# Experts: the inner-layer transposes and down products of a pair of blocks follow the next pair's gate and up products

## The reference, cut to what matters

```
def hier_moe(h, ...):            # N = 512 tokens, D = 1024, 2 experts each
    ... weight, eid = two best experts of the token's best group ...
    def expert_block(xb, e):
        return (silu(xb @ w_gate_e[e]) * (xb @ w_up_e[e])) @ w_down_e[e]   # 1024 -> 256 -> 1024
    y = sum over a token's two experts of weight * its row of the result
```

## Time and profile before

| | us |
|---|---|
| median of 3 runs | 3019.61 (3017.83 to 3027.75) |
| the profiled execution's own time | 3024.23 |
| its span | 3022.1 |

### The profile page before, as it was taken

One profiled execution on the slowest core, in us unless ns is written; L12 is line 12 of the kernel. 1 busy time (PEld: TensorE's weight loads), 2 busy tenths in 40 slices (PEclk: granted clock), 3 DMA queues, 4 the chain that ended last, 5 costly groups with the idle time before them and its releaser, 6 DMA issues.

```text
span 3022.1 us, 37947 instructions
## 1 busy us (share of the span) xinstructions
PE 2911.9 (96%) x15110; PEld 2272.2 (75%) x15110; DVE 1380.2 (46%) x2211; ACT 901.5 (30%) x1433; POOL 284.1 (9%) x318
## 2 busy tenths in 40 slices
PE   8999999999989999999999999999999988999995
PEld 7888888877846888888888888888888855864442
DVE  5646343545587565564333365333332277521113
ACT  4212111232176322223222244222233255321111
POOL 1000000001100100001000031000010155012221
PEclk9999999999999999999999999999999989999998
DMA  7232323221000365553222232232232200548985
GB/s 282 106 129 101 133 103 127 87 77 56 29 1 15 128 256 189 196 196 105 94 87 102 84 114 70 90 104 98 84 115 97 90 29 1 186 159 355 366 355 233
DMA packets 78350, 395.02 MB, mean 131 GB/s; under 512 B 17552, under 2 KB 19984, under 8 KB 51472
## 3 DMA queue, kind: packets, MB, share of 16 engines
q1 hardware_dynamic: 66704, 384.87, 34.4%
q0 software_dynamic: 11520, 8.43, 0.9%
HBM read 443.56 MB, written 16.78 MB: 152 GB/s over the span
## 4 chain that ended last, share of the span: by engine, by line
PE 90%; DVE 5%; ACT 2%; issue 1%; DMA 1%; POOL 1%; SPq 0%; DVEq 0%; ACTq 0%; POOLq 0%
PE ps L881 17%; PE ps L882 17%; PE ps L883 17%; PE ps L3176 5%; PE ps L3198 3%; PE ps L2210 2%; PE ps L2211 2%; PE ps L2212 2%; PE ps L1583 2%; PE ps L1602 1%; PE ps L1261 1%; PE ps L1262 1%; PE ps L1263 1%; PE ps L2972 1%; PE ps L2973 1%
## 5 line engine op out<-in xcount | busy, mean ns | idle before, releaser
L881 PE MATMUL ps<-h_high_ffn,weights_high_ffn 128*128 128x512 f32 (+1 forms) x1696 | 623.7, 368 | 1.9 <-DVE weights_low_ffn L1036 1.9
L882 PE MATMUL ps<-h_low_ffn,weights_high_ffn 128*128 128x512 f32 (+1 forms) x1696 | 623.8, 368 | 0.0
L883 PE MATMUL ps<-h_high_ffn,weights_low_ffn 128*128 128x512 f32 (+1 forms) x1696 | 623.3, 368 | 0.0
L881 PEld LDWEIGHTS ps<-h_high_ffn,weights_high_ffn 128*128 128x128 f32 x1696 | 320.1, 189 | 55.1 <-issue 2.4
L883 PEld LDWEIGHTS ps<-h_high_ffn,weights_low_ffn 128*128 128x128 f32 x1696 | 320.0, 189 | 52.7
L882 PEld LDWEIGHTS ps<-h_low_ffn,weights_high_ffn 128*128 128x128 f32 x1696 | 320.1, 189 | 52.2
L983 ACT ACTIVATE weights_high_ffn<-weights 128x2048 fp32r<-128x2048 f32 (+4 forms) x160 | 243.9, 1524 | 328.1 <-PE ps L883 263.7
L1036 DVE TENSOR_TENSOR weights_low_ffn<-weights,weights_high_ffn 128x2048 fp32r<-128x2048 f32 (+4 forms) x160 | 289.7, 1811 | 78.0 <-ACT weights_high_ffn L983 76.9
L881 PE MATMUL ps<-hidden_high_ffn,weights_high_ffn 128*128 128x512 f32 (+1 forms) x836 | 309.9, 371 | 0.8 <-DVE weights_low_ffn L1036 0.8
L882 PE MATMUL ps<-hidden_low_ffn,weights_high_ffn 128*128 128x512 f32 (+1 forms) x836 | 309.6, 370 | 0.0
L883 PE MATMUL ps<-hidden_high_ffn,weights_low_ffn 128*128 128x512 f32 (+1 forms) x836 | 309.4, 370 | 0.0
(11 more groups left out here) (479 smaller groups left out, 4499.8 us busy)
## 6 DMA issues: line engine op xcount, KB each, us to landing
weights<-in_ffn_gu SPq DMA_DIRECT2D x88, 1024.0 KB, 4.9
big<-in_w_exp_gu SPq DMA_DIRECT2D x32, 2048.0 KB, 13.2
scratch_ffn<-in_w_mod SPq DMA_DIRECT2D x35, 1536.0 KB, 6.5
weights<-in_ffn_d SPq DMA_DIRECT2D x24, 768.0 KB, 4.2
weights<-in_w_in SPq DMA_DIRECT2D x16, 1024.0 KB, 4.8
weights<-in_ffn_d SPq DMA_DIRECT2D x24, 640.0 KB, 3.9
weights<-in_w_exp_dn SPq DMA_DIRECT2D x15, 1024.0 KB, 18.3
hbuf<-in_w_exp_dn SPq DMA_DIRECT2D x12, 1024.0 KB, 19.4
```

The lines of the kernel that those rows point to most:

```text
L881: pe.matmul(out, wh, xh, start=(k == 0), stop=False)
L882: pe.matmul(out, wh, xl, start=False, stop=False)
L883: mm = pe.matmul(out, wl, xh, start=False, stop=(k == n - 1))
```

## The change

In PE's and ACT's order, `hidden_turn` and `down` of pair n now come after `gate_up(n + 1)`, with `turn(n + 2)` between the two. DVE has the same lag, with `hidden_turn` of the older pair ahead of `gate_up` of the newer one. On POOL the extra pair's gate-and-up loads are split from its down loads. They stand before the write of pair n - 1's result, and the down loads after it.

```
         def in_order(turn, gate_up, hidden_turn, down):
             turn(0)
-            for n in range(NP):
-                gate_up(n)
+            for n in range(NP + 1):
+                if n < NP:
+                    gate_up(n)
+                if n > 0:
+                    hidden_turn(n - 1)
                 if n + 1 < NP:
                     turn(n + 1)
-                hidden_turn(n)
-                down(n)
+                if n > 0:
+                    down(n - 1)
...
-                def load_extras(n):
+                def extra_gate_up(n):
                     for j in (2 * n, 2 * n + 1):
                         (wait for gate_up(n - 2), ask for the block's gate and up)
+                def extra_down(n):
+                    for j in (2 * n, 2 * n + 1):
                         (wait for the slot's down products, ask for the block's down)
                 for n in range(NP):
+                    extras = n + 2 < NP and SEQ[n + 2] >= EXPERTS // 2
                     if n + 2 < NP:
                         gpsimd.wait_ge(rows_turned.sem, n + 1)
                         gather_rows(gpsimd, n + 2)
+                    if extras:
+                        extra_gate_up(n + 2)
                     if n > 0:
                         scatter_rows(n - 1)
-                    if n + 2 < NP and SEQ[n + 2] >= EXPERTS // 2:
-                        load_extras(n + 2)
+                    if extras:
+                        extra_down(n + 2)
                 scatter_rows(NP - 1)
...                                             (DVE)
                 turn(0)
-                for n in range(NP):
-                    gate_up(n)
-                    hidden_turn(n)
+                for n in range(NP + 1):
+                    if n > 0:
+                        hidden_turn(n - 1)
+                    if n < NP:
+                        gate_up(n)
                     if n + 1 < NP:
                         turn(n + 1)
-                    down(n)
+                    if n > 0:
+                        down(n - 1)
```

More of the change, by code:

```diff
@@ L3128, in load_extras @@
                             .then_inc(extra_gu_landed[j % 2].sem, 16)
+                def extra_down(n):
+                    for j in (2 * n, 2 * n + 1):
+                        c = ORDER[j] - EXPERTS
                         if j >= DN_SLOTS:
```

## The result

The changed kernel takes 3028.59 us in the median (3021.02 to 3038.24, 20 runs), the kernel before 3021.86 us (3016.5 to 3027.75, 20 runs) in the same comparison. The ratio is 1.0021, with a 95% interval of 1.0013 to 1.0028. It is some 6 us slower, inside the 0.3% that was called "no change", and beyond its measurement's own uncertainty. The forecast was 3021.3 against 3019.6, +1.7 us; its own range of 3014 to 3028 (-6 to +8) and that of eight in ten (3008 to 3032) hold the ratio.

A forecast was written before the change was run, and what follows sets the result against it. Weights, not PE, were taken to set the experts' pace from the second round on. Start -3.2, first round -0.9, end +2.4, clock +3.4 gave +1.7 us: 3019.6 to 3021.3, own range 3014 to 3028, eight in ten 3008 to 3032.

The forecast's parts named there:

- L: Round of three pairs: first pair's (A's) weight request (T) to second pair's (B's) gate-and-up landing; 28.9 us, later 30.1 to 31.35.
- What bounds the kernel: Experts: weights set the pace from the second round on; rounds take 37.7 us, PE's own pace needs 37.14.
- Inner transposes and down products a pair later: Experts on PE: 0.57 us a pair saved, but waits for the second pair's weights, 1.6 to 2.9 us a round.
- Does L get shorter?: Weight transfers in the experts: L taken as unchanged; all six at 30.1 would give about -3 us, at 31.35 about +5.
- First round: Start of the experts: second pair's gate and up no longer follows the first's down products, -3.2 us; next round -0.9.
- The end: After the second-to-last pair's gate and up: put-off down products take 20.4 us instead of 18.0, +2.4 us.
- Extra weights asked for ahead of the write: POOL's order in the experts: protects against a wait and gains nothing; 0, upper end 1 us a round, 7 in all.
- The clock: Second pair's gate and up after its wait: two falls of 1.7 us, +3.4; bounds none and six, 0 to 10 us.
- The clock falls behind every wait: Rival, second pair's gate and up: six falls give +8.5 us, 3028, middle 3032; chance 0.17 including another loop loss.
- PE's pace wins: Rival, experts: L falls and PE's saving counts in full, -16.1 us, 3003.5; chance 0.15, wholly or more than half.
- Late rows: Rival, row gather behind write and down loads: lands after its transposes are due, up to +7 us; within the 0.68 for no change.

The follow-up runs named there:

- the last experiment: The kernel before, old step order, with SP asking for the first pair's down weights only after the second pair's gate-and-up weights: 3069.23 us against 3022.36, ratio 1.0158.

## Why the prediction was right, point by point

The forecast, no change that can be told, came true, and so did its mechanism: the weights set the pace, PE's gain turns into waits, and some of these bring the clock down. The sum did less well. The experts were to cost 1.7 us more and cost 8.4 in the first pair of profiles, 3.7 in the second; the ratio of the medians gives 6. That the first pair's spans differ by 6.1 and not by more is chance, 2.6 us of earlier stages. The six later rounds carry most of it: +3.4 forecast, +8.4 measured, of which 5.1 are falls of the clock and 3.3 a longer L.

*What bounds the kernel.* Right. The weights set the pace from the second round on, and 0.57 us a pair could not be had from PE alone. With half the weights the same step order gives 13 to 17 us; with all of them in the old request order it gives nothing.

*Inner transposes and down products a pair later.* Right in kind: PE's 0.84 us are gone and a wait ahead of each B has come in their place. The waits are 1.8 us in the first round, where 28.9 against 28.4 made it 0.5, and 2.5 to 3.7 in the six later ones, where 1.6 to 2.9 was said. PE's own round is 35.1, not 35.4.

*Does L get shorter?* It gets longer. The step "In both orders two gathers and two result writes fall into L" is wrong. The writes asked for within L of the second round, in the kernel before and in the changed one:

```profile
pair_rows<-work,slot_rows POOLq DMA_INDIRECT x2, 10.8
pair_rows<-work,slot_rows POOLq DMA_INDIRECT x3, 7.7
```

Before, L held B's gather and B's write, and those of X, which has almost no rows. The lag of one pair brings A's write in as well, which used to fall before T. The software queue's traffic in L shows it: 0.64 and 0.89 MB. In the first round L grew from 28.9 to 29.9 (29.8 in a second profile), so the -0.9 us forecast there were +0.1. In the later rounds it grew by 0.1 to 0.5 us each, 1 to 3 us in all. That A's write is the cause of this growth is argued and not shown: in the second round L did not grow with it, and with twelve products ahead of B it was 30.4.

*First round.* -3.1 us for the start, -3.2 forecast.

*The end.* +3.0 us, +2.4 forecast. `hidden_turn(22)` has no row transposes beside it, so DVE's copy (0.28) and the way to PE (0.14) show.

*Extra weights asked for ahead of the write.* 0 forecast; undone, it makes no difference that the time can tell, and alone 1.0009 with an interval that holds 1.

*The clock.* Two falls forecast, three in the profile, two in a second one, each 1.7 us as taken. Of the 8.4 us that the experts lost in the first profile 5.1 are the clock's. With twelve products in the wait no fall is left, with six one, and the ratio goes from 1.0021 to 1.0008 and 1.0007; these intervals overlap with the changed kernel's, so the times alone don't prove the gain. The Trainium skill ("TensorE: Matmul & The Clock Gate", section HAM oscillation) tells of a kernel in which every product step behind its wait for weights began cold; here four of seven waits brought no fall, and five of seven in the second profile.

*The rivals.* "The clock falls behind every wait" did not hold: two and three of seven waits brought a fall. The measured median lies near its 3028 only because L grew as well, which that rival left at its length. "PE's pace wins" fell. Late rows were nowhere seen: PE waits ahead of no row transposes.

## What to carry to other kernels

Where a transfer's slot is freed by the very products that the next transfer feeds, the step's time is a closed loop: request to landing, plus those products. Here work taken off the engine elsewhere gave nothing, and bytes taken out of the queue ahead of the late transfer gave 20 us. When an engine's order is changed so that something is needed later, change the order of the requests with it, and count the bytes of every queue, not the transfers, that move with the lag.

## What the runs showed of the hardware

A fall of the clock is not a matter of the wait's length alone: in one trace the waits of 2.84, 2.93 and 3.71 us brought one, those of 3.15, 2.60 and 2.46 us none; in a second trace of the same kernel one of 2.76 us did and one of 3.48 us did not. In the last experiment it fell at every one of seven waits, of 3.6 to 6.0 us. A 128x128 fp32 product of the identity took 0.25 us in a row of twelve, while eight transposes of the same size took 1.09 us together. With row gathers and result writes among the weights the DMA engines held 391 GB/s at a share of 0.99 over a whole round (397 without its first 0.7 us). And the indirect transfers bring many small packets: in L of the second round of the kernel before, 157 of the software queue's 638 packets were rows of 4 KB and 481 were of 4 bytes, by their number those of rows that name no token or expert, which is argued and not shown.
